# A modulation vector moved from TensorE to GpSimd, and a block inverse whose two forms are updated from one product

## What is computed

```python
# second block: the modulation vector, six pieces of 1024
cond = jax.nn.silu(c)                       # (1, 1024)
mod = cond @ mod_w[l] + mod_b[l]            # mod_w: (1024, 6144), 24 MB
sh1, sc1, g1, sh2, sc2, g2 = jnp.split(mod, 6, axis=-1)
# first block: h = rms_norm(x); mix = hgrn_rwkv_mixer(h, ...); x = x + mix
x = x + jnp.square(jax.nn.relu(h @ w_up[l])) @ w_down[l]
```

## Time and profile before

| | us |
|---|---|
| median of three runs | 1403.77 (1403.49 to 1404.30) |
| span of the profiled execution | 1399.9 |
| PE busy | 1186.8 (85%) |
| DVE busy | 593.1 (42%) |
| ACT busy | 436.0 (31%) |
| POOL busy | 22.6 (2%) |

### The profile page before, as it was taken

The page is one execution under the profiler, slowest core; times in us unless marked ns, Lnnn a source line. Parts: engine busy times, 40 slices in busy tenths (PEclk is TensorE's granted clock), DMA queues, the critical chain, the costliest instruction groups (busy, mean ns, idle before and its releaser), DMA issues.

```text
span 1399.9 us, 19232 instructions
## 1 busy us (share of the span) xinstructions
PE 1186.8 (85%) x8218; PEld 868.8 (62%) x8218; DVE 593.1 (42%) x971; ACT 436.0 (31%) x689; POOL 22.6 (2%) x45
## 2 busy tenths in 40 slices
PE   6999989999999999999999999898664745647477
PEld 6998756699887787589988777654321312213132
DVE  5688413576643675366644548833100101001011
ACT  4653320344433585354433431543010000000001
POOL 4000000000000000000000000000000000000000
PEclk9999999999999999999999999999787868878699
DMA  8352669355554555145554624777999999999997
GB/s 274 132 205 97 211 214 360 128 181 181 189 207 174 204 180 180 61 162 185 185 190 151 228 88 152 270 297 299 426 427 430 427 428 428 429 427 431 427 422 281
DMA packets 103052, 362.98 MB, mean 259 GB/s; under 512 B 7844, under 2 KB 13296, under 8 KB 92096
## 3 DMA queue, kind: packets, MB, share of 16 engines
q1 hardware_dynamic: 100736, 357.64, 66.2%
q0 software_dynamic: 2096, 4.17, 1.1%
q10 hardware_dynamic: 144, 0.07, 0.0%
HBM read 360.81 MB, written 1.05 MB: 258 GB/s over the span
## 4 chain that ended last, share of the span: by engine, by line
PE 61%; DMA 22%; DVE 5%; issue 2%; ACT 2%; SPq 1%; DVEq 0%; ACTq 0%
PE bank L935 33%; DMA arena<-in_exp_w 20%; PE bank L637 8%; PE bank L1049 3%; PE bank L907 3%; PE bank L917 2%; PE bank L1242 2%; PE bank L874 2%; PE bank L1589 1%; DMA ring<-in_exp_w 1%; SPq L2843 1%; PE bank L1259 1%; PE bank L1273 1%; PE bank L1287 1%; PE bank L1456 1%
## 5 line engine op out<-in xcount | busy, mean ns | idle before, releaser
L637 PE MATMUL bank<-arena 128*32 128x512 f32 x880 | 187.2, 676 | 69.6 <-DMA arena<-in_exp_w 69.6
L1740 DVE TENSOR_TENSOR low_w<-ring,split_high 128x2048 fp32r<-128x2048 f32 x84 | 189.6, 2288 | 104.3 <-ACT split_high L2438 104.2
L935 PE MATMUL bank<-turned_high,low_w 128*128 128x256 f32 x720 | 204.6, 284 | 0.0
L2438 ACT ACTIVATE split_high<-ring 128x2048 fp32r<-128x2048 f32 x84 | 157.8, 1917 | 136.5 <-DMA ring<-in_w_down 67.7
L637 PE MATMUL bank<-ring,arena 128*32 128x512 f32 x528 | 98.1, 721 | 82.0 <-DMA arena<-in_exp_w 80.9
L935 PE MATMUL bank<-turned_high,split_high 128*128 128x256 f32 x512 | 145.9, 285 | 3.0 <-DVE turned_low L1755 3.0
L935 PE MATMUL bank<-turned_low,split_high 128*128 128x256 f32 x512 | 144.9, 283 | 0.0
L935 PEld LDWEIGHTS bank<-turned_high,low_w 128*128 128x128 f32 x720 | 139.1, 193 | 0.0
L637 PEld LDWEIGHTS bank<-arena 128*32 128x32 f32 x880 | 47.7, 123 | 128.8 <-issue 128.6
L789 DVE TENSOR_TENSOR arena<-arena,bank 128x512 f32<-128x512 f32 x8 | 5.5, 687 | 271.1 <-PE bank L637 243.2
L637 PEld LDWEIGHTS bank<-ring,arena 128*32 128x32 f32 x528 | 27.2, 129 | 148.5 <-issue 147.4
(11 more groups left out here) (469 smaller groups left out, 1924.2 us busy)
## 6 DMA issues: line engine op xcount, KB each, us to landing
arena<-in_exp_w SPq DMA_DIRECT2D x51, 2048.0 KB, 23.6
ring<-in_exp_w SPq DMA_DIRECT2D x33, 2048.0 KB, 19.1
ring<-in_w_up SPq DMA_DIRECT2D x16, 2048.0 KB, 9.0
ring<-in_w_down SPq DMA_DIRECT2D x16, 2048.0 KB, 7.8
ring<-in_mod_w SPq DMA_DIRECT2D x12, 2048.0 KB, 8.5
arena<-in_exp_w SPq DMA_DIRECT2D x33, 512.0 KB, 13.8
ring<-in_w_in_ar SPq DMA_DIRECT2D x6, 2048.0 KB, 8.2
ring<-in_w_qkv SPq DMA_DIRECT2D x6, 2048.0 KB, 7.9
```

Source lines behind the costliest of these rows:

```text
L637: last = nc.tensor.matmul(mb[bank][strip(e), :], act[:, k, strip(e)], w[e][:, k, cols], start=(k == 0), stop=(k == n_k - 1), skip_group_ch ...
L935: last = mm(dst, *pair, start=(start and i == 0), stop=(stop and i == 2))
L1740: v.tensor_tensor(low_of(name, s), half_of(slot(name), name, s), high_of(name, s).bitcast(F32), ALU.subtract).then_inc(sem("split_low"), 1)
L2438: nc.scalar.activation(high_of(name, s), half_of(slot(name), name, s), ACT.Copy)\
```

## The change

1. The twelve 2 MB units of `mod_w` leave the ring, and the twelve `modulation` calls leave TensorE. GpSimd loads 48 pieces of 128 by 1024 (512 KB) through its own queue into two buffers in `spare`. It multiplies each by its column of `cond` and adds it to an accumulator, `mod_acc`, one for each chunk c of 1024 outputs, two of them by turns. Pieces 0 and 1 wait for `tilded`, and before piece 2 GpSimd waits for the last product of `w_in` 3 and loads the masks for the inverse. The transfer of piece i+2 is issued after piece i.
2. TensorE sums an accumulator over its 128 partitions in `mod_part(c)`, two matmuls against a strip of ones. Parts 0 and 1 stand in the chunks t of RWKV after `sa`, parts 2, 3 and 4 after `up` units 1, 4 and 7 of the first feed-forward layer, and part 5 after the first half of its `down`. VectorE takes each into `mod_sum` (`take_mod`), where ScalarE copied the whole before.
3. In the inverse's levels 2 to 32 a product `xx` = `near_invT` (as weights) times `a_inv` takes the place of the turn by the identity. It stands between `ax` and `xax`, and VectorE writes its masked entries into `near_inv`. ScalarE no longer copies turned groups. The masks for both forms come from a table made on the host.
4. Four semaphores are merged into one (`scales_ready`), with the waits at the same places.

```diff
-    whole(("mod",), a["mod_w_2"][0], MOD_UNITS)
...
+        mod_piece = [spare[:, 2048:3072], spare[:, 3072:4096]]
+        mod_acc = [spare[:, 1024:2048], big_row_t[:, :]]
...
-            pe.wait_ge(sem("cond_ready"), 1)
-            mod_bank = banks.hold(pe, "mod")
-            def modulation(*units_):
-                for c in units_:
-                    w = blocks(weights(pe, "mod", c), KC)
-                    for k in range(KC):
-                        strip = slice(STRIP * (k % 4), STRIP * (k % 4 + 1))
-                        at = MOD_UNITS - 1 - c
-                        last = mm(mod_bank.ap[strip, :], cond3[:, k, at:at + STRIP], w[:, k, :],
-                                  start=(c == 0 and k < 4), stop=(c == MOD_UNITS - 1 and k >= 4), skip_group_check=True)
-                    if c < MOD_UNITS - 1:
-                        last.then_inc(sem("mod_read"), 1)
-                        unit_read[("mod", c)] = (sem("mod_read"), c + 1)
-                    else:
-                        last.then_inc(mod_bank.full, 1)
-                        read_by(mod_bank, "mod", c)
+            def mod_part(c):
+                pe.wait_ge(sem("mod_step"), KC * (c + 1))
+                bank = banks.take(pe, "mod_part", c)
+                for n in range(2):
+                    u = 2 * c + n
+                    at = MOD_UNITS - 1 - u
+                    last = mm(bank.ap[STRIP * (u % 4):STRIP * (u % 4 + 1), :], one_strip[:, at:at + STRIP],
+                              mod_acc[c % 2][:, n * 512:(n + 1) * 512], start=True, stop=True, skip_group_check=True)
+                last.then_inc(bank.full, 1)
             pe.wait_ge(sem("inv_first"), 1)
...
-            near_turn(1)
...
-                    banks.wait_read(pe, "x", LEVELS[n], g)
+                    if n:
+                        banks.wait_read(pe, "xx", LEVELS[n], g)
+                    else:
+                        banks.wait_read(pe, "x", g)
                     bank = banks.take(pe, "ax", m, g)
...
-                modulation(n)
+                if m < 64:
+                    for g in range(4):
+                        banks.wait_read(pe, "ax", m, g)
+                        if n:
+                            banks.wait_read(pe, "xax", LEVELS[n], g)
+                        bank = banks.take(pe, "xx", m, g)
+                        for i in range(4):
+                            at = slice(i * 64, (i + 1) * 64)
+                            for b in BLOCKS:
+                                last = mm(bank.ap[b, at], near_invT[b, 4 * g + i, :], a_inv[b, 4 * g + i, :],
+                                          start=True, stop=True)
+                        last.then_inc(bank.full, 1)
                 for g in range(4):
-                    banks.wait_read(pe, "ax", m, g)
+                    if m == 64:
+                        banks.wait_read(pe, "ax", m, g)
+                        banks.wait_read(pe, "xax", LEVELS[n], g)
                     bank = banks.take(pe, "xax", m, g)
...
-                if m < 64:
-                    near_turn(m)
...
-                modulation(6 + 3 * t)
...
-                modulation(7 + 3 * t)
+                mod_part(t)
                 banks.wait_read(pe, "sa", t)
...
-                modulation(8 + 3 * t)
...
+                    if l == 0 and c in (1, 4, 7):
+                        mod_part(2 + c // 3)
...
+                    if l == 0 and n == 0:
+                        mod_part(MOD_CHUNKS - 1)
...
+            dve.wait_ge(sem("near_masks_landed"), 16)
             for m in LEVELS[1:]:
+                if m < 64:
+                    for g in range(4):
+                        bank = banks.read(dve, "xx", m, g)
+                        v.copy_predicated(near_inv[:, 4 * g:4 * g + 4, :], mid(near_mask(m, False), 4).bitcast(I32),
+                                          blocks(bank.ap[:, 0:256], 4)).then_inc(bank.freed, 1)
                 for g in range(4):
                     bank = banks.read(dve, "xax", m, g)
...
+            def take_mod(c):
+                bank = banks.read(dve, "mod_part", c)
+                own = mod_rows(c)
+                if c < 2:
+                    step(v.tensor_copy(mod_sum[own], bank.ap[own, :]))
+                else:
+                    step(v.tensor_tensor(mod_sum[own], mod_sum[own], bank.ap[own, :], ALU.add))
+                v.memset(next(flag), 0.0).then_inc(bank.freed, 1)
...
+                take_mod(t)
...
-            keep_quarter(near_inv, slice(0, P), "x", 1)
+            keep_quarter(near_inv, slice(0, P), "x")
...
-                if m < 64:
-                    keep_quarter(near_inv, slice(0, P), "x", m)
...
-            evacuate(mod_sum[:, :], ACT.Copy, "mod")
...
+            def load_mod(i):
+                c, k = i // KC, i % KC
+                pool.dma_start(mod_piece[i % 2], a["mod_w_2"][0][k * P:(k + 1) * P, c * D:(c + 1) * D])\
+                    .then_inc(sem(f"mod_landed{i % 2}"), 16)
+            load_mod(0)
+            load_mod(1)
+            pool.wait_ge(sem("cond_ready"), 1)
+            pool.wait_ge(sem("tilded"), 1)
+            for i in range(KC * MOD_CHUNKS):
+                c, k = i // KC, i % KC
+                acc, piece = mod_acc[c % 2], mod_piece[i % 2]
+                if i == 2:
+                    banks.read(pool, "in", 3, 1)
+                    pool.dma_start(xn[:, 1024:1024 + NEAR_COLS], a["constants"][:, n_const:n_const + NEAR_COLS])\
+                        .then_inc(sem("near_masks_landed"), 16)
+                if k == 0 and c >= 2:
+                    banks.read(pool, "mod_part", c - 2)
+                pool.wait_ge(sem(f"mod_landed{i % 2}"), 16 * (i // 2 + 1))
+                scaled = acc if k == 0 else piece
+                last = nc.gpsimd.tensor_scalar(scaled, piece, cond[:, k:k + 1], None, ALU.mult)
+                if k > 0:
+                    last.then_inc(sem("mod_scaled"), 1)
+                    pool.wait_ge(sem("mod_scaled"), i - c)
+                    last = nc.gpsimd.tensor_tensor(acc, acc, piece, ALU.add)
+                last.then_inc(sem("mod_step"), 1)
+                pool.wait_ge(sem("mod_step"), i + 1)
+                if i + 2 < KC * MOD_CHUNKS:
+                    load_mod(i + 2)
+            banks.read(pool, "mod_part", MOD_CHUNKS - 1)
```

More of the change, by code:

```diff
@@ L44 @@
 MOD_UNITS = 12
+MOD_CHUNKS = MOD_UNITS // 2
 MOD_ROWS = [4, 5, 10, 11]
@@ L1251, in _ @@
-            pe.wait_ge(sem("inv_first"), 1)
-            def near_turn(m):
-                for g in range(4):
-                    if m > 1:
-                        banks.wait_read(pe, "xax", m, g)
-                    bank = banks.take(pe, "x", m, g)
-                    for i in range(4):
-                        for b in BLOCKS:
-                            last = mm(bank.ap[b, i * 64:(i + 1) * 64], near_invT[b, 4 * g + i, :], ident[b, b],
-                                      start=True, stop=True)
-                    last.then_inc(bank.full, 1)
@@ L2080, in feed_forward @@
                             .then_inc(sem("act_ready"), 1)
+                    if l == 0 and c in (1, 4, 7):
+                        take_mod(2 + c // 3)
                 for n in range(2):
@@ L2084, in feed_forward @@
                     add_to_x("down", l, ns=(n,), scale=rstd2)
+                    if l == 0 and n == 0:
+                        take_mod(MOD_CHUNKS - 1)
                 turned_lows(("x_gate", l), range(KC // 2))
```

63 lines of the change are left out of this document (35 added, 28 removed).

## The result

| | before | after |
|---|---|---|
| median of the comparison | 1403.63 us | 1466.71 us (1462.14 to 1470.16, 4 runs) |
| span of the profiled execution | 1399.9 us | 1468.3 us |
| ratio | | 1.0445, 95% interval 1.0416 to 1.0473 |

The change makes the kernel 63 us slower. The forecast was 1421 us, with a range up to 1446, so the sign was that of the forecast and the size was far off. Where the 68.4 us between the two profiled spans arise is seen by setting the same four places of the program side by side. The second place is where part 5 of `mod_part` begins, behind the first half of `down`; in the kernel before it is where that half ends.

What follows compares the result with a forecast made beforehand. TensorE was taken to bound the early stretches, the experts' weight transfers the end. -17.0 + 1 + 3 + 30 = +17 us on 1399.9 gives 1416.9, and with the median 3.9 above the span 1421 us; own range 1408 to 1446, overall from 1383.

Steps and rivals of the forecast that it cites:

- Parts 1 to 3: On TensorE: modulation leaves (-24.6 us), uncovered waits +1.2 and +1.0, inverse 0, `mod_part` +5.4; sum -17.0 us.
- to the end in full: Any gain or loss ahead of 447 us moves the experts' weight-bound stage as a whole, so all of it reaches the end.
- Part 4, the pace: GpSimd takes 4.5 us a piece, at the slow end 5.6; TensorE's wait at `mod_part(1)` costs +1 us.
- Part 5, the turns: GpSimd and VectorE take turns reading SBUF: +3 us ahead of the first `up`, +30 us through late `low_w`.
- Slow but free: Rival: 5.6 us a piece, VectorE undisturbed, waits eat the gain: -2 us, 1402; chance 0.08, shared with turns eating the gain.
- Free engines: Rival: VectorE and GpSimd don't disturb each other, 4.5 us a piece: -18 us, 1386; chance 0.42, including a too-quick GpSimd.
- Heavy turns: Rival: engines take turns with GpSimd passes of 2.2 us each, over by about 50: 1441; chance 0.50 together with the forecast.
- The inverse's levels: Sign: levels of 5.6 us where they were 7.5, from `inv_first` to `w_out` 21 to 22 us shorter.
- `mod_part` ending idle time: Sign: in the feed-forward layer `mod_part` should end idle time of TensorE.
- longer L1740: Sign: VectorE's L1740 group in the feed-forward layer shows idle time or longer spans beside GpSimd's passes; 2288 ns unchanged refutes turns.
- A wait at part 1 of over 3 us would refute the pace: Sign: TensorE waiting over 3 us at `mod_part(1)` would refute GpSimd's 4.5 us a piece.
- The 133 us: Sign: the window from the first `up` product to the end of `down`'s first half, 133 us, should become about 163.

Runs made afterwards that it cites:

- the loads alone: The changed kernel with GpSimd's arithmetic left out: it loads all 48 pieces and only clears accumulator columns; 1399.63 us, ratio 0.9979 to the kernel before.
- VectorE's version: The changed kernel with GpSimd only issuing loads, VectorE multiplying and adding pieces in idle places, sums asked for later; 1401.68 us, ratio 0.9973, repeated 1400.49 us, 0.9983.

## Why the prediction was wrong

**The sum, term by term.** The forecast was -17 + 1 + 3 + 30 = +17 us, at 1421 us, and the measured time is 1466.71. At part 5 of `mod_part` the changed kernel is 59.6 us behind the one before. By the loads alone TensorE would be there at 394.5 us and not at 403.9: -9.4. GpSimd undisturbed would have its last piece at 419 us, worked out from the trace: the 17th piece begins at 231.55, and 26 pieces of 6.22, four of 3.8, one of 5.4 (it issues no transfer) and a last of 5.3 follow. That is 24.5 us behind 394.5. The last add really ends at 463.5, so what happens beside VectorE adds 44.5. The sum is -9.4 + 24.5 + 44.5 = 59.6. The 419 is an estimate; no run had GpSimd's arithmetic undisturbed.

**Parts 1 to 3, TensorE's saving (mechanism right, size too high).** The loads alone bring `w_out` forward by 14.5 us where the sum gave 20.6. `mod_part` was taken at 0.9 us and measured 0.98 at the upper clock and 1.85 at the lower. The copies of the inverse hide; the levels last 6.0 us where 5.6 was written. What fails is that the gain would go "to the end in full": 14.5 us became 8.3 and then 3.7. The four later parts of `mod_part` explain 4 of the first 6.2; the rest, and the 4.6 between the embedding and the end, no run here explains.

**Part 4, the pace (the step that failed first).** The term was +1 us and is about 24.5. The price of a pass was bounded by VectorE's 1.22 us at one end and twice that at the other, which gave 5.6 us a piece as the slowest case and 4.5 as the value. A piece took 6.22 us with nobody in the way. The issue and the handovers were right (0.61 + 0.4 against 1.0), the add is 1.9 of VectorE's passes, and the product is 2.3. At 6.22 the formula gives 143.3 + 14 x 6.22 - 0.7 = 229.7 us for part 1's last piece, and the trace has that add end at 230.6. That it comes so near is partly luck: it leaves out that GpSimd starts 2.4 us after 143.3 and that a chunk's first piece has no add, and the two cancel. TensorE had stood there for 16.8 us where the term was 1, and so the gain of 14.5 at `w_out` turned into a loss of 6.1 (the other 3.8 are there before this wait begins, at 213.8 us). The bound from the nearest row was not a bound: that a simpler operation is no slower on another engine was assumed.

The Trainium skill's figure (GPSIMD Engine Reference, section 3.1) was right for the add: 2.25 us estimated, 2.34 measured. Its section 4.1 calls one-input operations on GpSimd roughly line-rate, in line with the prediction's "a shorter pass for the one-input product". This case's trace differs: 2.85 us for 1024 columns with the column of `cond` as scalar, longer than the add. The measurement decides.

**Part 5, the turns (they are there, but size and path were wrong).** The term was +3 and +30 us, with VectorE late with `low_w` for TensorE. It is about 44.5, and in the changed kernel TensorE waits 1.9 us for `low_w` and 55.6 for GpSimd. The one that is held up to the end is GpSimd: its products last 4.10 us in the mean and not 2.85 (25 x 1.24 = 31 us in its group above), its adds lose about 9, and the rest is mainly waits for a piece to land (3.7). VectorE's own loss (12.6 + 10.2 + 6.0 + 6.3 = 35 us in its four groups) is largely hidden behind TensorE's waits for GpSimd. The prediction took the two engines as one sum of busy times against a window (83 + 77 against 133), so that only what didn't fit would cost; in truth every microsecond that GpSimd is held up moves its last piece, and comes on top of its pace.

The Trainium skill (SBUF — State Buffer, section Who interferes with whom) says that a VectorE instruction with two SBUF inputs and a GpSimd instruction that reads SBUF exclude each other, that casts in a two-port mode do so too, and that the order of issue decides who stands. The runs agree on the first two: adds stretch the squares from 688 to 1637 ns and the copies from 427 to 1313. Whether the order of issue decides isn't shown. That beside VectorE products are stretched by nearly half, and adds by a tenth, is measured here and not told there.

**The rivals.** "Slow but free" had the right path, TensorE waiting at `mod_part`, and said it decides from 4.7 us a piece on; with GpSimd done at 419 us it would give some 15 us over the kernel before, about 1419, and so it holds less than half of the loss. "Free engines" is refuted twice: by the pace, and by its own price, since with no arithmetic at all the time is 1400 and not 1386. "Heavy turns" at 1441 was the nearest, 26 us below. The forecast chose between pace and turns where both were at work.

**What it named as signs.** The inverse's levels, `mod_part` ending idle time, and longer L1740 all came. "A wait at part 1 of over 3 us would refute the pace" came as well, with 16.8 us. Part 0 was in time; part 3 waited for 2.4 us, part 4 for 25.6 and part 5 for 10.8. The 133 us from the first product of `up` to part 5 became 187 (276.9 to 463.5) and not 163.

What stays open: why the clock falls in the chunks, why the gain of the loads alone shrinks on the way to the end, and why VectorE's version varies by more than the kernel before.

## What to carry to other kernels

Work that leaves the bounding engine for an idle one must be priced by that engine's own rows for the same form of instruction; where there are none, the slow end of the range has to be far out, and the last due time checked against count times price before anything else. If that engine shares its memory access with another, what holds it up is added to its own chain, and not only to the other's. A faster helper isn't always better: a two-input form on GpSimd is shorter and costs VectorE more, so ask of each variant who stands still for it. Take the gain's best case (the arithmetic left out) first; here it was 3 or 4 us, which leaves GpSimd's work next to nothing to cost.

## What the runs showed of the hardware

- GpSimd over 128 by 1024 fp32, alone: an add of two tensors 2.34 to 2.36 us, a product by a per-partition column 2.85 us, the same product with the column broadcast as a second tensor 1.91 us. The form with fewer tensor inputs is the slowest.
- Idle adds on GpSimd cost the end of the program about 1.05 us each, for which nobody waits; idle products cost nothing that can be told from none (2 us for 30), but last 4.08 us each beside VectorE.
- The start of one GpSimd pass after another that it depends on takes about 0.1 us, and an issue of a transfer after a pass 0.30 us of handover and 0.53 to 0.61 us itself.
- Where TensorE's filler work was removed from a stretch of small dependent products, its granted clock was lower: in the 30 us ahead of `w_out` 0.94 before, 0.70 with the loads alone, and 0.50 with the arithmetic on VectorE, where TensorE was still busy for 29.11 of 30 us.
